# A streaming-encoder step: pace of the projection chain, ranks of one tile, and 24 ticks of the expert sum moved from DVE to PE

## The reference

```python
x = x + merge(o_sb, o_sw, o_mem, gates, w_o_sb, w_o_sw, w_o_mem, w_out)   # gates = sigmoid(h @ w_gate + b)
x = x + peer_ffn(rmsnorm(x, norm_ffn), w_peer_q, peer_keys, peer_u, peer_v)
# peer_ffn, per row and head (8 heads): q = xb @ w_q; scores against 2 x 128 keys; top 16 of each half,
# top 16 of the 256 sums -> 16 of 16384 experts; g = softmax(best)
a = gelu(einsum('thkd,td->thk', u_tab[idx], xb))
y = einsum('thk,thkd->td', g * a, v_tab[idx])
```

## Time and profile before

| | us |
|---|---|
| median of 3 runs (4054.07 to 4062.14) | 4054.19 |
| the profiled execution, its own time | 4089.85 |
| its span, which all rows below are in | 4088.0 |
| ticks 26 to 63 (1222.1 to 1471.4) | 249.3 |
| ticks 64 to 127 (1471.4 to 1875.0) | 403.6 |
| ticks 128 to 255 (1875.0 to 2677.1) | 802.1 |
| ticks 256 to 281 (2677.1 to 2851.0) | 173.9 |
| tick 282 to the last (2851.0 to 4075) | 1224.0 |

### The profile page before, as it was taken

The page is one execution under the profiler, slowest core; times in us unless marked ns, Lnnn a source line. Parts: engine busy times, 40 slices in busy tenths (PEclk is TensorE's granted clock), DMA queues, the critical chain, the costliest instruction groups (busy, mean ns, idle before and its releaser), DMA issues.

```text
span 4088.0 us, 40853 instructions
## 1 busy us (share of the span) xinstructions
PE 3374.4 (83%) x13885; PEld 1890.4 (46%) x13885; DVE 2752.4 (67%) x5752; ACT 1009.5 (25%) x2925; POOL 1625.1 (40%) x1327
## 2 busy tenths in 40 slices
PE   8999898989759997865979878720989999989998
PEld 4545665578423335432333433210555555555554
DVE  2131456611787786676988799779976888866667
ACT  2111557711333321312222232311111111111111
POOL 0000000000455557757557676776333333333332
PEclk9999889999879998887989989865999999999999
DMA  5911320034899976758989999999999999999998
GB/s 184 301 41 52 127 88 22 14 134 152 332 389 407 365 282 245 249 198 347 412 350 393 413 379 348 362 386 359 415 414 414 405 408 414 411 414 411 414 410 353
DMA packets 320096, 1248.31 MB, mean 305 GB/s; under 512 B 40320, under 2 KB 134784, under 8 KB 216064
## 3 DMA queue, kind: packets, MB, share of 16 engines
q0 software_dynamic: 141312, 872.69, 53.9%
q1 hardware_dynamic: 129408, 347.85, 22.6%
q10 hardware_dynamic: 49168, 25.17, 2.1%
HBM read 1190.33 MB, written 56.16 MB: 305 GB/s over the span
## 4 chain that ended last, share of the span: by engine, by line
PE 25%; DVE 24%; DMA 17%; issue 5%; POOL 4%; ACT 2%; another core or an unknown queue 1%; SPq 0%; DVEq 0%; ACTq 0%; POOLq 0%
DMA shared<-in_experts_dram 10%; PE ps L1616 8%; DVE ring L1996 8%; PE ps L1522 5%; PE ps L1605 3%; DMA ring<-in_experts_dram,idx 3%; PE ps L1654 3%; DVE o_x L1968 3%; PE ps L1547 2%; PE ps L1532 2%; DMA shared<-gates_scratch 2%; POOL gates_scratch L1471 2%; POOL ring L1458 2%; DMA s<-s_scratch 1%
## 5 line engine op out<-in xcount | busy, mean ns | idle before, releaser
L1458 POOL DMA_INDIRECT ring<-in_experts_dram,idx x768 | 956.8, 1246 | 1787.3 <-DVE o_x L1968 774.2
L1616 PE MATMUL ps<-shared 128*128 128x512 f32 x1536 | 692.0, 601 | 86.4 <-DMA shared<-in_experts_dram 75.6
L1996 DVE CUSTOM_DVE_ANT_0 ring<-ring,xp 128x1024 f32<-128x1024 f32 x512 | 634.4, 1272 | 126.8 <-DMA ring<-in_experts_dram,idx 86.9
L1751 ACT ACTIVATE act_<-hid 128x2 f32<-128x2 f32 x448 | 91.0, 203 | 2138.7 <-DVE hid L1996 2012.6
L1654 PE MATMUL ps<-ring,diag 64*64 64x512 f32 x2816 | 409.6, 696 | 243.9 <-ACT diag L1769 216.0
L1605 PE MATMUL ps<-shared 128*128 128x256 f32 x2048 | 467.1, 381 | 150.7 <-ACT shared L1737 145.2
L1605 PEld LDWEIGHTS ps<-shared 128*128 128x128 f32 x2048 | 391.1, 191 | 260.8 <-issue 205.5
L1968 DVE SCALAR_TENSOR_TENSOR o_x<-ring,wgt,o_x 128x1024 f32<-128x1024 f32 x384 | 491.7, 1280 | 0.1
L1616 PEld LDWEIGHTS ps<-shared 128*128 128x128 f32 x1536 | 290.1, 192 | 423.0 <-issue 405.9
L1996 DVE CUSTOM_DVE_ANT_0 ring<-ring,mixn 128x1024 f32<-128x1024 f32 x384 | 469.6, 1223 | 18.4 <-DMA ring<-in_experts_dram,idx 15.2
L1522 PE MATMUL ps<-shared 128*128 128x256 f32 (+2 forms) x1152 | 411.7, 506 | 38.8 <-DMA shared<-hT_scratch 29.8
(11 more groups left out here) (208 smaller groups left out, 3653.8 us busy)
## 6 DMA issues: line engine op xcount, KB each, us to landing
shared<-in_u_blocks_dram SPq DMA_DIRECT2D x128, 512.0 KB
shared<-in_experts_dram SPq DMA_DIRECT2D x128, 512.0 KB
shared<-in_w_gate_o_dram SPq DMA_DIRECT2D x72, 768.0 KB
gates_scratch<-vsw ACTq DMA_DIRECT2D x1, 24576.0 KB, 124.3
shared<-in_w_q_dram SPq DMA_DIRECT2D x24, 1024.0 KB
shared<-gates_scratch SPq DMA_DIRECT2D x128, 192.0 KB
shared<-in_w_out_dram SPq DMA_DIRECT2D x12, 1024.0 KB
ring<-in_experts_dram,idx POOLq DMA_INDIRECT x768
```

The costliest lines, as they stand in the source:

```text
L1458: i = nc.gpsimd.indirect_dma_start(out=row, out_offset=None, in_=A["u_rows"] if valued(j) else A["experts"], in_offset=bass.IndirectOffset ...
L1616: last = nc.tensor.matmul(ps[:, BANKS[a] + h, :], given, dv[:, v % 3, h * HB:(h + 1) * HB], start=False, stop=(b == NK - 1), skip_group_ch ...
L1996: last = nc.vector.tensor_tensor_reduce(out=u, in0=u, in1=rows, scale=1.0, scalar=0.0, op0=ALU.mult, op1=ALU.add, accum_out=hid[:, j % SLO ...
```

## The change

- `Front.weight`: the steps of groups 1 and 2 are spread so that each tick gets about the same sum of weights. For group 1 a gate step weighs 2.67, an out step 3.6, a query step 4.8, the tail 3.5, other steps 1.5. Group 2 keeps equal weights.
- `LEADS`: group 1's chain begins with 2 empty steps (weight 3 each), group 2's with 6. SP asks for the inputs in step 0; PE's first gate step comes after the empty ones.
- The ranks of tile 1 go from ticks 30 to 77 into ticks 28 to 61; its first four merges go from ticks 57 to 60 into 48 to 51, the other four from 81 to 84 into 65 to 68.
- The held sum begins at slot 48 of tile 6 instead of slot 0. The slots of ticks 256 to 279 (`whole`) are summed on PE: ACT writes a full 128 x 128 diagonal (two buffers of it in place of four small ones) and PE does two products with 512 columns each into `acc`. DVE adds `acc` to the tile's rows once, at the first held slot, and only then counts `y_ready`; the dense stage's seeds wait for that.

```diff
+HELD_AT = HELD_FROM * SLOTS + 48
+def whole(j):
+    return HELD_FROM * SLOTS <= j < HELD_AT
 def held(j):
-    return j >= HELD_FROM * SLOTS
+    return j >= HELD_AT
+LEADS = (0, 2, 6)
...
-        self.out_at = 3 * KC * Y + 3
+        lead = self.lead = LEADS[g]
+        self.out_at = lead + 3 * KC * Y + 3
-        self.unit = {u * Y + y: (u, y) for u in range(3 * KC) for y in range(Y)}
+        self.unit = {lead + u * Y + y: (u, y) for u in range(3 * KC) for y in range(Y)}
...
+    def weight(self, tau):
+        if self.final:
+            return 1.0
+        if tau < self.lead:
+            return 3.0
+        if tau in self.unit:
+            return 8.0 * self.n / self.Y / 3
+        if tau in self.out:
+            return 3.6
+        if tau in self.query:
+            return 1.2 * self.n
+        return 3.5 if tau >= self.q_at else 1.5
...
+    def spend(f, at, first, last):
+        weights = [f.weight(tau) for tau in range(f.steps)]
+        reached = [sum(weights[:tau + 1]) / sum(weights) for tau in range(f.steps)]
+        for i in range(first, last):
+            share = min(1.0, (i + 1 - first) / (last - 4 - first))
+            yield at + sum(x <= share + 1e-9 for x in reached)
...
+    for f, first, last in ((FRONTS[1], RANK_LEAD, 2 * NB), (FRONTS[2], 2 * NB, 4 * NB)):
+        for to in spend(f, total[f.g - 1], first, last):
...
-RANK_AT = {1: (30, 48), 3: (2 * NB + 2, 28), ...
+RANK_AT = {1: (28, 34), 3: (2 * NB + 2, 28), ...
...
-                pe.wait_ge(y_ready, len(PE_TILES))
+                pe.wait_ge(y_ready, len(PE_TILES) + 1)
...
+                if whole((n * NB + q) * BATCH):
+                    pe.wait_ge(diags, len(PE_TILES) * NB + q + 1)
+                    if q == 0:
+                        pe.wait_ge(y_ready, len(PE_TILES))
+                    for j in range((n * NB + q) * BATCH, (n * NB + q + 1) * BATCH):
+                        d = by_pe(j) - 1
+                        for h in range(2):
+                            last = nc.tensor.matmul(acc[:, h, :], diag[:, 2 * (d % 2):2 * (d % 2) + 2, :].rearrange("p a b -> p (a b)"),
+                                                    ring[:, j % RING, DM + h * HB:DM + (h + 1) * HB],
+                                                    start=(j == HELD_FROM * SLOTS), stop=(j == HELD_AT - 1), skip_group_check=True)
+                        last.then_inc(pe_done, 1)
...
+                        if whole(j):
+                            act.wait_ge(pe_done, max(d - 1, by_pe(HELD_FROM * SLOTS - 1)))
+                            last = nc.scalar.activation(diag[:, 2 * (d % 2):2 * (d % 2) + 2, :].rearrange("p a b -> p (a b)"), ident, ACT.Copy,
+                                                        scale=wgt[:, j % SLOTS:j % SLOTS + 1])
+                            continue
...
-                if j == HELD_FROM * SLOTS:
+                if j == HELD_AT:
                     dve.wait_ge(resid, f.outs0 + 4 * f.n)
+                    dve.wait_ge(pe_done, by_pe(HELD_AT - 1))
+                    link(nc.vector.tensor_tensor(x1, x1, acc.rearrange("p a n -> p (a n)"), ALU.add))
+                    dve.sem_inc(y_ready, 1)
```

More of the change, by code:

```diff
@@ L1026, in __init__ @@
         self.steps = self.q_at + 4 * PH + 12
-        self.unit = {u * Y + y: (u, y) for u in range(3 * KC) for y in range(Y)}
-        self.tanh = {u * Y + Y + 1: u for u in range(3 * KC)}
-        self.mix = {u * Y + Y + 2: u for u in range(3 * KC)}
+        self.unit = {lead + u * Y + y: (u, y) for u in range(3 * KC) for y in range(Y)}
+        self.tanh = {lead + u * Y + Y + 1: u for u in range(3 * KC)}
+        self.mix = {lead + u * Y + Y + 2: u for u in range(3 * KC)}
         self.out = {self.out_at + i: (i // n, i % n) for i in range(4 * n)}
@@ L1077, in paces @@
     out = [done]
[L1078 to L1083, removed]
+    def spend(f, at, first, last):
[4 more added lines that the diff above has]
+            yield at + sum(x <= share + 1e-9 for x in reached)
+    start = done
+    for i in range(RANK_LEAD):
+        to = start + -(-(total[0] - start) * (i + 1) // RANK_LEAD)
         out.append(to - done)
         done = to
[L1086 to L1090, removed]
+    for f, first, last in ((FRONTS[1], RANK_LEAD, 2 * NB), (FRONTS[2], 2 * NB, 4 * NB)):
+        for to in spend(f, total[f.g - 1], first, last):
+            out.append(to - done)
+            done = to
+    out.extend([0] * (DENSE_AT - 4 * NB))
     ticks = len(SEQ) * NB - DENSE_AT
@@ L1099 @@
 PACES = paces()
-RANK_AT = {1: (30, 48), 3: (2 * NB + 2, 28), 4: (2 * NB + 34, 28), 5: (2 * NB + 66, 28), 7: (4 * NB + 8, 36), 8: (5 * NB + 6, 48)}
+RANK_AT = {1: (28, 34), 3: (2 * NB + 2, 28), 4: (2 * NB + 34, 28), 5: (2 * NB + 66, 28), 7: (4 * NB + 8, 36), 8: (5 * NB + 6, 48)}
 RANKED = {at + length * c // (3 * PH): (m, c // 3, c % 3) for m, (at, length) in RANK_AT.items() for c in range(3 * PH)}
@@ L1410, in store @@
                     return
-                if held(n * SLOTS):
+                if n >= HELD_FROM:
                     f = FRONTS[-1]
-                    sp.wait_ge(y_ready, n)
+                    sp.wait_ge(y_ready, n + 1)
                     sp.dma_start(YS[SEQ[n]], x1_of(f, SEQ[n] - f.base)).then_inc(y_out[n % 2], 16)
@@ L1441, in _ @@
             store(len(SEQ) - 1)
-            sp.wait_ge(y_ready, len(SEQ) - 1 + NV)
+            sp.wait_ge(y_ready, len(SEQ) + NV)
             for a in range(NV):
@@ L1492, in _ @@
                     elif held(j):
-                        pool.wait_ge(d_held, j - HELD_FROM * SLOTS + 1)
+                        pool.wait_ge(d_held, j - HELD_AT + 1)
                     elif valued(j):
@@ L1769, in _ @@
                         last = nc.scalar.activation(diag[:, d % 4, :], folded, ACT.Copy, scale=wgt[:, j % SLOTS:j % SLOTS + 1])
-                    if n in PE_TILES:
+                    if n in PE_TILES or whole((n * NB + q) * BATCH):
                         last.then_inc(diags, 1)
@@ L1961, in hold @@
                 x1 = x1_of(f, SEQ[j // SLOTS] - f.base)
-                if j == HELD_FROM * SLOTS:
+                if j == HELD_AT:
                     dve.wait_ge(resid, f.outs0 + 4 * f.n)
+                    dve.wait_ge(pe_done, by_pe(HELD_AT - 1))
+                    link(nc.vector.tensor_tensor(x1, x1, acc.rearrange("p a n -> p (a n)"), ALU.add))
+                    dve.sem_inc(y_ready, 1)
                 if j % BATCH == 0:
                     dve.wait_ge(acted, 2 * (j // BATCH) + 2)
-                if j % SLOTS:
-                    dve.wait_ge(d_held, j - HELD_FROM * SLOTS)
+                if j > HELD_AT:
+                    dve.wait_ge(d_held, j - HELD_AT)
                 last = nc.vector.scalar_tensor_tensor(out=x1, in0=ring[:, j % RING, DM:2 * DM], scalar=wgt[:, j % SLOTS:j % SLOTS + 1], in1=x1,
@@ L1971, in hold @@
                 if j % SLOTS == SLOTS - 1:
-                    dve.wait_ge(d_held, j - HELD_FROM * SLOTS + 1)
+                    dve.wait_ge(d_held, j - HELD_AT + 1)
                     dve.sem_inc(y_ready, 1)
@@ L2017, in _ @@
                         merge(*MERGED[T])
-                    if q == 0 and n and not held((n - 1) * SLOTS) and n - 1 != VALUED:
+                    if q == 0 and n and n <= HELD_FROM and n - 1 != VALUED:
                         finish(n - 1)
```

## The result

The changed kernel takes 4070.51 us (median of 7 runs, 4062.49 to 4072.47), the kernel before 4054.09 (7 runs, 4047.99 to 4067.51): ratio 1.0032, 95% interval 1.0017 to 1.0048. By the ratio it is slower by 0.3%, 13 us (the two medians are 16 us apart). I had predicted 15 us faster.

A forecast was written before the change was run, and what follows sets the result against it. PE was taken to bound ticks 26 to 63, DVE 264 to 281, DMA 128 to 263 and from 282. Terms -6 (+24, -30), -2, -11, +4 gave -15: from median 4054.2 to 4039 us, range 4005 to 4069.

The forecast's parts named there:

- Sum 374 against 403.6: -30: Ticks 64 to 127: stage times after group 1's new spread add to 374 us against 403.6 profiled, saving 30.
- the other four terms: Ticks 26 to 63 +24 us, leads -2, sum on PE -11, the part from tick 282 on +4.
- Rival 2: Query ticks 98 to 116: the "remote" waits aren't PE's and stay; 15 us come back, 4054 in all; chance 0.15.
- Ticks 26 to 63, +24: Eleven more gate steps lengthen PE-bound ticks by 29.7 us, less 6 for POOL's wait; bounds +20 to +40.
- rival 1: All smoothing kept: ticks 26 to 63 only +12, ticks 64 to 127 -46, sum -14.5; 4010 us; chance 0.22.
- The queries' pace, 5.6 us a tick: Query ticks 88 to 116: POOL's four transfers a tick set the pace, DVE close behind, PE no longer; 28.5 ticks, 160 us.
- Leads, −2: Group 2's lead, ticks 128 to 255: little effect in a DMA-bound stretch, bounds -10 to +8; group 1's lead: nothing.
- The sum on PE, −11 and +4: Ticks 264 to 281 save 11 us as DVE is relieved; from tick 282 late seeds and first scores cost 4.
- Rival 4: PE stays cold in ticks 256 to 279: 182 us in place of 161, whole 4071 us; chance 0.07.
- the 0.7 us a tick: Sum on PE: allowance, from 0 to 1 us a tick, for waits between PE and ACT with only two diagonals held.
- Rival 3: Early ticks overfilled: ticks 26 to 63 +40, ticks 64 to 127 -20, rest -7; 4067 us; chance 0.12.

The follow-up runs named there:

- e5: Kernel before with only the weighted spread of groups 1 and 2; no leads, early ranks or sum on PE: 4081.47 us, ratio 1.0058.
- e7: Kernel before with the sum on PE and 58 gate steps up to tick 63, the rest spread later; ranks as before, no leads: 4021.23 us, ratio 0.9900.
- e6: Kernel before with only the ranks of tile 1 moved early, into ticks 28 to 61: 4080.17 us, ratio 1.0051.
- e9: Changed kernel with the lead of group 2 alone, group 1's removed: ratio 0.9990 against the kernel before.
- e4: Changed kernel without any leads: ratio 1.0027 against the kernel before.
- e8: Changed kernel with tile 1's scatters two in every tick instead of four a tick in four ticks of every eight: 4083.76 us, ratio 1.0056.
- e13: Kernel before with the weighted spread for group 1 alone, group 2 rounded up as before: 4065.77 us, ratio 1.0017.
- e2: Kernel before with only the sum on PE; spread, leads and ranks as before: 4048.42 us, ratio 0.9983.
- e3: Changed kernel without the sum on PE, keeping spread, leads and early ranks: 4079.09 us, ratio 1.0052.

## Why the prediction was wrong

**The step that failed: "Sum 374 against 403.6: -30".** The 374 for the changed kernel was good (369.6). The 403.6 it was set against was not the kernel's time but one execution's: the kernel before takes 372 to 375 in these ticks. The gain was 3.8 us, 26 less than the sum had; the other four terms were off by −0.5, +5.7, −3.1 and −1.6, which nearly cancel. With 373.5 as its base this term is next to nothing and the same sum gives +15 to +16, where the timed runs show 13. All four stretches that I had named for the changed kernel (273, 374, 800, 163) came within 5 us; only what they were set against was wrong. The 374 itself owes something to luck: its gate ticks (64 to 74) took 74.6 us for 66, its out steps and norm (75 to 87) 67.8 for 82.

Two signs stood in the rows. The profiled execution was 35.7 us above the median, and I subtracted the 15 from the median as if the excess lay evenly; and ACT's 44.0 us of "remote" waits in the earlier trace rows had no line of the kernel behind them. I explained them as missing PE records. Rival 2 named them and took them for something permanent that would stay; they were in no other profile. What stalled that execution stays open.

**Ticks 26 to 63, +24: size right (+23.5) by luck, cause only in part.** I charged 11 x 2.70 us on PE and took nothing for DVE. Already the 11 was wrong: it sets 75 steps by the schedule against 64 counted in the window. By the schedule it is 75 for 66, in the window 73 for 64: nine. And a step had no fixed price: ten more cost 2 to 5 us (e5), less even than rival 1's +12, while PE's waits for diagonals fell from 17.7 to 1.8 us; seven fewer gave 22 (e7). Why the two sides differ so isn't shown. The rest of the +23.5 is the ranks (+17 alone, e6) and group 1's lead (+10, e9 against after). I had the ranks only as the upper end of the bounds and the lead at nothing. The parts don't add up: ranks and weights together give +13 (e4, 263.6). In the changed kernel, PE's sum waits 15.4 us, DVE is busy 215.7 us and DMA is down to 0.89:

```profile
L1692 PE MATMUL ps<-ring,diag 64*64 64x512 f32 x460 | 64.7, 665 | 15.4 <-ACT diag L1812 15.4
```

**The queries' pace, 5.6 us a tick: right, with its cause.** Ticks 98 to 116 take 107.2/19 = 5.64 us; PE is busy 86.2 us, DVE 92.7, and POOL issues all the time (its lines under e8), as forecast. But the tick was 6.6 us before, and not 7.45; there PE was the bound.

**Leads, −2: wrong by its cause.** Group 1's costs about 15 us, group 2's gives about as much, but only against its own rounding. I had written that group 2's steps would come "five ticks later" in a stretch bound by DMA and change nothing; e5 and e13 show that this stretch answers to the tick in which single steps come: 810.1 against 793.8 us. DMA at 0.95 to 0.97 busy did not hide them.

**The sum on PE, −11 and +4: −14.1 and +2.4.** DVE falls to 82.1 us, DMA rises to 0.96. Lines of ticks 264 to 281, answering to the earlier trace rows:

```profile
L1674 PE MATMUL ps<-ring,diag 128*128 128x512 f32 x131 | 68.7, 672 | 22.7 <-ACT diag L1807 22.7
L1485 POOL DMA_INDIRECT ring<-in_experts_dram,idx x38 | 44.3, 1165 | 27.0 <-DVE o_x L2014 10.3 <-PE ps L1674 9.4 <-issue 7.3
L1807 ACT ACTIVATE diag<-const,wgt 128x128 f32<-128x128 f32 x32 | 12.1, 398 | 15.0 <-PE ps L1674 14.4
```

The timeline of PE shows in some runs of ticks the two handovers at 0.49 us and a tick every 4.19 us (4.2 forecast), in others longer waits (over the 24 ticks a burst comes every 6.0 us), and after the last tick summed on PE the seeds:

```profile
2770.43 3.70 PE L1674 MATMUL ps<-ring,diag 128*128 128x512 f32 x8 [0.49 <-ACT diag L1807]
2774.62 3.70 PE L1674 MATMUL ps<-ring,diag 128*128 128x512 f32 x8 [0.49 <-ACT diag L1807]
2778.81 3.70 PE L1674 MATMUL ps<-ring,diag 128*128 128x512 f32 x8 [0.49 <-ACT diag L1807]
...
2815.21 7.99 PE L1623 MATMUL ps<-shared,const 128*128 128x512 f32 x12 [9.01 <-DVEq L2009]
```

**Rival 4 came in six ticks of 24, and not in the time:** the stretch took 159.6 us, not 182, with the granted clock at 0.89 and 0.86 and PE 64 and 70% busy. It is a mixture. Behind waits of 0.49 us the clock stayed at 1.00, and the 8 products of a tick took 3.70 us. But after PE had stood for 4.38, 4.38 and 4.57 us, three bursts began at a granted clock of 0.50 (the lower level, 1.2 GHz) and took 6.38, 6.66 and 6.09 us. One of them, its first 3 us, and four bursts at full clock:

```profile
2739.94 6.38 PE L1674 MATMUL ps<-ring,diag 128*128 128x512 f32 x8 [4.38 <-ACT diag L1807]
```

```profile
2739.94:2743.00 3.06, 3.06 (x4) 1.51 (x5) 2.52 (x5) 0.23 (x2) 2.45 (x3) 0.50 1.01 410
2770.43:2787.16 16.73, 14.80 (x32) 5.74 (x32) 9.58 (x25) 4.18 (x15) 13.02 (x13) 1.00 0.86 317
```

Three more bursts took 5.40 us, behind waits of 4.09, 4.66 and 2.15. That is 13 us more of PE time in all; how much of it reached the stretch wasn't separated. By the Trainium skill (TensorE: Matmul & The Clock Gate, HAM oscillation) PE falls back to half clock in a long wait between bursts, so that the next burst starts slow. This trace agrees for the three bursts behind the waits of 4.4 to 4.6 us; those behind 0.49 us, near the 0.7 us a tick that I had allowed for, ran at full clock.

**Rival 3** is where the time came out (4067 against 4070.5), and its condition held: +23.5 in ticks 26 to 63 is more than 3.8 + 14.1. Its prices, +40 and −20, were both too large.

## What to carry to other kernels

A stretch of one profile is a term of a sum only if that execution is a usual one: set its own time beside the median first, and if it is tens of us above, find the excess (waits that no line explains, a tick of 20 us where its neighbours take 4 to 10) before a change is credited with removing it. Before work is moved for evenness, rank the stretches by the air of all engines together: here PE and DMA were both 0.93 busy in ticks 26 to 63, and moving seven gate steps out of them, on top of the sum on PE, brought the ratio from 0.9983 (e2) to 0.9900 (e7), where moving nine in with the ranks and leads lost 0.5% (e3). A DMA share of 0.96 doesn't hide everything else; check the rounding of a schedule as well as its weights. Count steps before and after by the same measure.

## What the hardware showed

- Executions of the same code agree to 0.1 us in 278 of the 421 ticks from 26 to 446 (all three profiles of the kernel before), and yet one had about 30 us more in ticks 64 to 127 than the other two, 26 of them in four ticks, in one of which PE, ACT and DVE stood for some 10 us while POOL issued.
- Issuing an indirect transfer took POOL 1.1 to 1.2 us and 0.3 us of issue before it. Four a tick set the pace of the query ticks at 5.64 us.
- Scatters in bursts (four a tick in four ticks of eight) beat two in every tick by 8 us in 19 ticks (107.2 against 115.5), one execution of each; the ratios are 1.0032 and 1.0056.
- The order of single PE steps moved a stretch with DMA at 0.95 to 0.97 by 16 us in 800 (e5 against e13).
- Bursts of 8 products that took 3.70 us at granted clock 1.00 took 6.1 to 6.7 us when they began at 0.50, after PE had stood for 4.4 to 4.6 us.
